# Ten expert slots and three weight-panel buffers, where there were eleven and two

## What is computed

```python
q = (xt @ w_q).reshape(PEER_BLOCK, PEER_HEADS, 2, PEER_DK // 2)
s = jnp.einsum('thcd,hcnd->thcn', q, keys, preferred_element_type=jnp.float32)
sv, si = lax.top_k(s, PEER_TOPK)
...
idx = jnp.take_along_axis(cand_i, top_p, axis=-1)
g = jax.nn.softmax(top_s, axis=-1)
a = jnp.einsum('td,thkd->thk', xt, u_tab[idx], preferred_element_type=jnp.float32)
hk = (g * jax.nn.gelu(a, approximate=False)).astype(xt.dtype)
return jnp.einsum('thk,thkd->td', hk, v_tab[idx])
```

## Time and profile before

| | |
|---|---|
| median of three executions | 3516.58 us |
| the profiled execution: time, span | 3523.25 us, 3521.2 us |
| granted TensorE clock, mean | 0.939 |
| TensorE, VectorE, ScalarE, GpSimd busy | 87%, 65%, 33%, 38% |
| moved by DMA, mean over the span | 1245.70 MB, 354 GB/s |
| first gather, last gather issued | 461.9 us, 3448.1 us |

### The profile page before, as it was taken

One profiled execution on the slowest core, in us unless ns is written; L12 is line 12 of the kernel. 1 busy time (PEld: TensorE's weight loads), 2 busy tenths in 40 slices (PEclk: granted clock), 3 DMA queues, 4 the chain that ended last, 5 costly groups with the idle time before them and its releaser, 6 DMA issues.

```text
span 3521.2 us, 32961 instructions
## 1 busy us (share of the span) xinstructions
PE 3059.3 (87%) x9362; PEld 1708.0 (49%) x9362; DVE 2275.9 (65%) x5803; ACT 1171.7 (33%) x3492; POOL 1339.2 (38%) x1106
## 2 busy tenths in 40 slices
PE   8987679898988799999898899999996578888886
PEld 7744545444543356555553455655463244433333
DVE  0255667777557877778767767764675688777452
ACT  0014223233323443333333452322332244434331
POOL 0010034453434444434435334444544335445451
PEclk9998889999998899999999899999998799999998
DMA  4241189999999999999899899999999899999995
GB/s 185 96 156 48 60 341 421 378 421 380 421 420 421 384 411 415 421 421 404 349 420 422 339 401 378 416 410 409 421 420 243 319 379 370 409 379 398 421 421 219
DMA packets 179495, 1245.70 MB, mean 354 GB/s; under 512 B 20425, under 2 KB 24009, under 8 KB 31985
## 3 DMA queue, kind: packets, MB, share of 16 engines
q0 software_dynamic: 156160, 1111.70, 79.6%
q1 hardware_dynamic: 23008, 130.85, 9.4%
q10 hardware_dynamic: 144, 1.05, 0.1%
HBM read 1237.09 MB, written 6.46 MB: 353 GB/s over the span
## 4 chain that ended last, share of the span: by engine, by line
PE 51%; DVE 21%; DMA 15%; ACT 4%; issue 3%; DVEq 3%; another core or an unknown queue 2%; ACTq 1%; POOL 0%; POOLq 0%; SPq 0%
PE acc L1479 28%; DMA arena<-in_uv,idx 14%; DVE arena L1281 9%; PE bank L1504 8%; PE bank L1496 6%; PE bank L1317 3%; ACT diag L907 1%; ACT act_w L900 1%; PE bank L1344 1%; DVEq L1211 1%; PE bank L1390 1%; ACT L891 1%; DVE ya L1147 1%; DVE yb L1148 1%
## 5 line engine op out<-in xcount | busy, mean ns | idle before, releaser
L1479 PE MATMUL acc<-arena,diag 128*128 128x512 f32 x4160 | 1950.9, 625 | 333.3 <-ACT diag L907 331.8
L720 POOL DMA_INDIRECT arena<-in_uv,idx x1024 | 1280.2, 1250 | 1820.3 <-PE acc L1479 1533.7
L1281 DVE CUSTOM_DVE_ANT_0 arena<-arena,h 128x1024 f32<-128x1024 f32 x1024 | 1210.4, 1221 | 434.2 <-DMA arena<-in_uv,idx 432.6
L1479 PEld LDWEIGHTS acc<-arena,diag 128*128 128x128 f32 x4160 | 820.6, 200 | 1346.2 <-issue 948.3
L897 ACT ACTIVATE act_w<-dots 128x4 f32<-128x4 f32 x260 | 53.4, 205 | 1552.7 <-DVE dots L1281 1545.8
L1504 PE MATMUL bank<-hT,panel 128*128 128x256 f32 (+1 forms) x1792 | 408.3, 383 | 0.9 <-ACT hT L858 0.9
L1504 PEld LDWEIGHTS bank<-hT,panel 128*128 128x128 f32 x1792 | 338.5, 190 | 81.3 <-issue 34.5
L907 ACT ACTIVATE diag<-cst,act_w 128x128 f32<-128x128 f32 x1040 | 341.8, 391 | 96.0 <-PE acc L1479 77.0
L900 ACT ACTIVATE act_w<-act_w 128x1 f32<-128x1 f32 x1040 | 221.5, 283 | 22.0 <-issue 1.1
L1496 PE MATMUL bank<-panel,hT 128*128 128x256 f32 (+1 forms) x640 | 146.2, 383 | 2.7 <-DMA panel<-in_panels 1.8
L897 ACT ACT_TABLE_LOAD x109 | 139.8, 1283 | 1.1
(11 more groups left out here) (185 smaller groups left out, 2288.7 us busy)
## 6 DMA issues: line engine op xcount, KB each, us to landing
panel<-in_panels SPq DMA_DIRECT2D x109, 1024.0 KB
arena<-in_uv,idx POOLq DMA_INDIRECT x1024
arena<-in_cache_k POOLq DMA_DIRECT2D x16, 512.0 KB, 4.6
arena<-in_cache_v POOLq DMA_DIRECT2D x16, 512.0 KB, 4.5
lng<-in_ln SPq DMA_DIRECT2D x6, 512.0 KB
lnb<-in_ln SPq DMA_DIRECT2D x6, 512.0 KB
h<-in_h SPq DMA_DIRECT2D x1, 2048.0 KB
out_nv_p<-arena POOLq DMA_DIRECT2D x4, 512.0 KB, 10.4
```

Of the source, the lines that this page charges most:

```text
L720: nc.gpsimd.indirect_dma_start(uv[:, e % SLOTS_UV, :], None, uv_dram[layer], bass.IndirectOffsetOnAxis(ids[:, r:r + 1], 0)).then_inc(gathe ...
L1281: V.tensor_tensor_reduce(uv[:, e % SLOTS_UV, 0:D], uv[:, e % SLOTS_UV, 0:D], x_rows, 1.0, 0.0, ALU.mult, ALU.add, dots[:, G % 2, r:r + 1]) ...
L1479: m = mm(acc[:, half * 512:(half + 1) * 512], diag[:, r % DIAGS, :], uv[:, e % SLOTS_UV, D + half * 512:D + (half + 1) * 512], start=False ...
```

## The change

The expert ring gets ten slots and the weights get three panel buffers. A slot is 2 x 1024 numbers in each partition and a panel is 8 x 256, both 8 KB, so the memory taken stays what it was. `SLOTS` also sets the number of panel semaphores. The attention's tiles still fit the smaller arena (19,537 of 20,480 numbers in a partition). SyncE issues panel 2 at the start, ahead of the constants.

```diff
@@ -50,7 +50,7 @@
-SLOTS_UV = 11
+SLOTS_UV = 10
@@ -62,7 +62,7 @@
 PW = 256
-SLOTS = 2
+SLOTS = 3
 BANKS = 4
@@ -643,6 +643,7 @@
             load_panel(0)
             sp.dma_start(h0T_late, h0T[:, :, G_W[0]:T]).then_inc(s_hT, 16)
             load_panel(1)
+            load_panel(2)
             sp.dma_start(cst[:], consts[:, 0:N_CONST]).then_inc(s_const, 16)
```

## The result

The changed kernel took 3543.5 us (median of four, 3540.5 to 3545.7) where the kernel before took 3515.5 (3513.9 to 3523.3): ratio 1.0065, interval 1.0053 to 1.0078, so 0.65% or 23 us slower. The ratio rests on 21 executions of the changed kernel, with a median of 3540.5 us; the two medians of four would give 1.0080, or 28 us.

The account below looks back on a forecast made before the run. From 462 us the DMA bounds it, in a loop of slots, gathers, dots and products. Ring +11.2, third buffer -4.7, panel traffic 0: +6.5 us on 3516.6, 3523 us; overall range 3509 to 3545, forecast's own 3509 to 3527.

Parts of the forecast that it names:

- Where the loss is: Expert phase: DMA averages 396 GB/s against 421, 178 us short of full, 126 us of it dips with all eleven slots full.
- the ring's term: Cost of ten slots at eight places where full DMA stretches begin: 11.2 us, bounds 0 and 19.9 us.
- crossing: Passage from TensorE giving back a slot, over issuing its gather, into back-to-back gathers; eight, each costing 0 to 2.49 us.
- the sum: Ring cost, third buffer's gain and panel traffic: 11.2 - 4.7 + 0 = +6.5 us, so 3523 us on the median's scale.
- Rival (a): Each of the eight stretches of gathers starts a full gather late: +15.2 us net, 3532 us, slower by 0.43%; 27%.
- Where gathers queue behind each other this costs nothing.: In full DMA stretches the lost slot is free: five gathers queued keep a DMA engine as busy as six.
- Rival (b): GpSimd's gather issues fall into VectorE's dots, held up to 4.3 us longer each; four such holds give 3549 us; 15%.
- The third buffer's gain: Last stretch, after the last expert: TensorE's two waits for a panel go, -4.7 us, bounds 0 to 4.7.
- The panels among the gathers, costed at 0: Panels issued earlier in the expert phase add to one stretch and leave another: 0 together, bounds -2.5 and +2.5 us.
- (d): Burst at 3446 us adds a panel among the last gathers: last landing 2.5 us later, 3526 us; part of the forecast's case.
- Three signs of the prediction: Profile after: last gather 6 to 20 us later, expert-phase rate down one or two GB/s, end 4.7 us shorter.
- (c): The third panel moves into each of the eight DMA dips: -13.4 us, 3503 us, faster; 8%.

## Why the prediction came out as it did

**Where the loss is.** The loop of slot, gather, dot, product and slot bounds the kernel, and losing a slot costs where the DMA runs dry: this held. So did the split of the change into a ring that costs and a third buffer that gives a little back. Ten slots alone are about as slow as the change.

**The size of the ring's term.** This step failed. I took 11.2 us, and ten slots alone measured 25 (32 by the wait alone, and 23.5 in the changed kernel's trace at the last dot). I had priced each crossing by the depth of its dip, with half a gather for the middling ones and nothing for the shallow. The eight dips that I priced lose 53 us together, of the 126 that I had worked out for all dips; the other 73 had no term. The largest step, at 2150 us, lies there. Nor had the sum a term for TensorE's clock: 2.8 us of that step are products that ran at the lower level behind a longer wait. Rival (a), the full gather at all eight, gives 19.9 and is nearer; its forecast of 1.0043 is still under the interval.

**"Where gathers queue behind each other this costs nothing."** This is the second part of the same failure. I had looked at how many gathers are outstanding in the last stretch, six or so. Which batch a gather waits for stands in the kernel: gather e needs `slot_done >= e - SLOTS_UV + 1`, and the slots come back in fours. With twelve slots all four gathers of a quarter wait for the same batch. With eleven the fourth waits for the next one, with ten the third does too, with nine the second. The rows at 2150 us show what it costs when the third does. How often it costs at each depth wasn't counted, so that a slot is worth 9, then 25 to 32, then 34 to 39 us is measured and not derived.

**Rival (b), gathers issued into the dots.** It has a part in the largest step: at 2150 us a gather that was issued clear of the dots is issued into them and held for 5.19 us. As a general cause it falls. The mean issue didn't rise, it fell from 1.250 to 1.232 us, and issues over 3 us are 12 before, 10 in the changed kernel, 7 and 8 in the two others with ten slots and 5 with nine. How much of the 3.8 us the hold itself made is open: to try it, VectorE's dots would have to leave GpSimd's issues alone, and that wasn't tried.

**The third buffer's gain.** The two waits went, as predicted, 4.7 us, and the last panel's products ran at the higher clock, 1.8 us: 6.5 together. The term was right in kind and too small. The other 1.9 of the 8.4 us between the two traces are products in front of any wait for a panel, and the largest part of them isn't the buffer's: the last expert products took 10.05 us before, 8.65 after, and 8.57 in ten slots alone. The kernel with its last panels in free slots has the gain without the rest, 7 us.

**The panels among the gathers, costed at 0.** This held, panel by panel. Against before, the changed kernel's delay falls by 1.6 us behind 2968 us, where the panel issued at 2980 is gone, grows by some 3 more than with ten slots alone at the burst, falls by 2.5 at 3350 us, where the next single panel is gone, and grows by 2.5 among the last gathers. With ten slots alone none of these four is there. They add up to about +1, within the bounds of -2.5 and +2.5, and (d) falls with them: the last gather does land later by one panel, and the one at 3350 us pays for it.

**The sum.** 25 for 11.2, -6.5 for -4.7 and +1 for 0 make some 20 us, and 23 (19 to 27) were measured. The measured ratio is slower than "no change that can be told". The range held the time (3543.5 in 3509 to 3545), but only because it had been stretched towards rival (b), which isn't the cause (and whose own 3549 us it leaves out): that is luck, and the likeliest case was wrong. Three signs of the prediction say so as well: the last gather came 23.5 us later and not 6 to 20, the rate fell by 3 GB/s and not by one or two, and the end grew shorter by more than 4.7 us.

**(c), that the third buffer fills the dips,** falls: ten slots alone and the whole change differ by less than can be told.

## What to carry to other kernels

In a ring of buffers that is given back in batches, count how many fetches of a batch hang on the next batch; the mean number outstanding doesn't show it. The price of a buffer is then measured by taking one away with the wait alone, which needs no memory. It doesn't tell what one more is worth: here taking one away cost 25 to 32 us, and one more gave 9.

A delay that a deep enough ring swallows can stay in a shallower one, and a wait that gets longer can cost TensorE's clock on top.

A loader in the shadow of a bandwidth-bound stream need not prefetch as early as it may. Here the panels of the last stretch were pulled out from among the last gathers, into slots that the ring had finished with, and that was worth more than the third buffer. The same delay for an earlier burst, with more gathers to come behind it, gave nothing that can be told.

## What the runs showed of the hardware

A gather's issue on GpSimd takes 0.94 us and up to 5.3 us if VectorE's dots run at that moment (5.19, 5.25 and 5.31 us in the rows above and the earlier trace rows). In the light version of the search VectorE lost 18% of its work in the expert phase, and the mean issue stayed at 1.24 us: that speaks for the dots, and not the search, as what holds it.

TensorE's clock took a part in the small numbers. The same sixteen products of the last panel took 5.41 us after a wait of 2.92 us and 3.62 us without it. Sixteen expert products took 9.88 us behind a gap of 5.49 us, and 7.13 behind one of 1.69. The length of the gap doesn't settle it: at 550 us they took 9.89 and 7.13 us behind gaps of 3.25 and 3.21 us.
